# Paired weight products: two pieces split by one operation, a ring of eight half slots

## The reference

```
first block:   x += 0.5 * swiglu(rmsnorm(x))       w_gu 1024 x 5632, w_down 2816 x 1024
               x += hybrid_mixer(rmsnorm(x))       w_in; short convolution, gated linear attention,
                                                   sigmoid gates ga, gb, silu gate r, w_o
               x += 0.5 * swiglu(rmsnorm(x))
               x  = rmsnorm(x)
second block:  x += (neighbourhood attention | retention) @ w_out
               x += square(relu(rmsnorm(x) @ w_up)) @ w_down     4096 wide
               x  = rmsnorm(x)
```

## Time and profile before

| | before |
|---|---|
| median of three runs | 1752.6 us |
| profiled execution | 1752.49 us |
| its span | 1750.3 us |
| TensorE busy | 1743.7 us, 100% |
| VectorE busy | 1180.2 us, 67% |
| ScalarE busy | 847.5 us, 48% |
| GpSimd busy | 201.8 us, 12% |

### The profile page before, as it was taken

How to read it: one execution, slowest core, us unless ns; L and a number is a source line. 1 busy time by engine, 2 the same in 40 slices (tenths; PEclk the granted TensorE clock), 3 DMA queues, 4 the chain that set the end, 5 groups by cost and what they waited for, 6 DMA issues and landing times.

```text
span 1750.3 us, 26650 instructions
## 1 busy us (share of the span) xinstructions
PE 1743.7 (100%) x10407; PEld 1534.1 (88%) x10407; DVE 1180.2 (67%) x1843; ACT 847.5 (48%) x1442; POOL 201.8 (12%) x262
## 2 busy tenths in 40 slices
PE   9999999999999999999999999999999999999998
PEld 7889989878888899988888998988877888989897
DVE  7848748666776546865794784876688677747474
ACT  6425526454333335743553562654655543727274
POOL 1002201000001012200110220200232010202000
PEclk9999999999999999999999999999999999999999
DMA  7247736332125355733445573634522253637352
GB/s 224 79 139 173 195 97 157 110 108 86 51 85 155 97 145 154 175 107 98 136 121 152 147 193 111 167 100 133 139 62 61 85 144 97 161 109 185 100 133 72
DMA packets 85451, 220.66 MB, mean 126 GB/s; under 512 B 10800, under 2 KB 12080, under 8 KB 85328
## 3 DMA queue, kind: packets, MB, share of 16 engines
q1 hardware_dynamic: 58512, 156.92, 29.1%
q0 software_dynamic: 25536, 59.97, 16.0%
q10 hardware_dynamic: 1280, 2.08, 0.3%
HBM read 214.74 MB, written 2.10 MB: 124 GB/s over the span
## 4 chain that ended last, share of the span: by engine, by line
PE 97%; DVE 1%; ACT 0%; issue 0%; DMA 0%; DVEq 0%; ACTq 0%; POOLq 0%
PE ps L2101 19%; PE ps L2103 19%; PE ps L2102 19%; PE ps L2193 10%; PE ps L2195 10%; PE ps L2194 10%; PE ps L2123 2%; PE ps L2125 2%; PE ps L2124 2%; PE ps L2342 0%; PE ps L2472 0%; PE ps L2497 0%; PE ps L2483 0%; PE ps L2345 0%; PE ps L2330 0%
## 5 line engine op out<-in xcount | busy, mean ns | idle before, releaser
L2101 PE MATMUL ps<-Ahi,wh 128*128 128x512 f32 x913 | 357.1, 391 | 0.0
L2102 PE MATMUL ps<-Alo,wh 128*128 128x512 f32 x913 | 355.3, 389 | 0.0
L2103 PE MATMUL ps<-Ahi,wl 128*128 128x512 f32 x913 | 355.3, 389 | 0.0
L2193 PE MATMUL ps<-BThi,wh 128*128 128x256 f32 x1232 | 340.2, 276 | 0.0
L2194 PE MATMUL ps<-BTlo,wh 128*128 128x256 f32 x1232 | 340.1, 276 | 0.0
L2195 PE MATMUL ps<-BThi,wl 128*128 128x256 f32 x1232 | 340.1, 276 | 0.0
L585 ACT ACTIVATE wh<-raw 128x1024 fp32r<-128x1024 f32 (+1 forms) x206 | 213.2, 1036 | 221.1 <-PE ps L2103 187.1
L1203 DVE TENSOR_TENSOR wl<-raw,wh 128x1024 fp32r<-128x1024 f32 (+1 forms) x206 | 250.2, 1215 | 64.4 <-ACT wh L585 62.3
L2194 PEld LDWEIGHTS ps<-BTlo,wh 128*128 128x128 f32 x1232 | 231.3, 188 | 0.0
L2193 PEld LDWEIGHTS ps<-BThi,wh 128*128 128x128 f32 x1232 | 231.3, 188 | 0.0
L2195 PEld LDWEIGHTS ps<-BThi,wl 128*128 128x128 f32 x1232 | 231.2, 188 | 0.0
(11 more groups left out here) (398 smaller groups left out, 2802.9 us busy)
## 6 DMA issues: line engine op xcount, KB each, us to landing
raw<-in_w_gu SPq DMA_DIRECT2D x96, 256.0 KB, 3.1
raw<-in_w_d SPq DMA_DIRECT2D x32, 512.0 KB, 4.2
raw<-in_w_dn SPq DMA_DIRECT2D x32, 512.0 KB, 4.1
raw<-in_w_gu SPq DMA_DIRECT2D x22, 512.0 KB, 3.8
raw<-in_w_up SPq DMA_DIRECT2D x36, 256.0 KB, 2.9
SS<-in_w_gu POOLq DMA_DIRECT2D x32, 256.0 KB, 5.1
tm<-in_w_gu POOLq DMA_DIRECT2D x32, 256.0 KB, 4.0
S1B<-in_w_gu POOLq DMA_DIRECT2D x32, 256.0 KB, 5.1
```

Of the source, the lines that this page charges most:

```text
L2101: pe.matmul(ps, wh[:, c], hi[:, k, :], start=(k == 0), stop=False)
L2102: pe.matmul(ps, wh[:, c], lo[:, k, :], start=False, stop=False)
L2103: last = pe.matmul(ps, wl[:, c], hi[:, k, :], start=False, stop=(k == nb - 1))
L2193: pe.matmul(ps, whi[:, w], bhi, start=(new and kp == 0), stop=False, skip_group_check=not new)
```

## The change

The seven pieces of a pair become five splits: b11; s1 and s2 together; b12; s3 and s4 together; b22. `STEP` says which split a product belongs to. One ScalarE copy and one VectorE subtraction of 1024 columns serve two pieces. For that, s1 (two buffers, for even and odd pairs) and s2 lie in one tensor SUM1 of three rows, s3 and s4 in SUM3; an operation reads two of the three rows. The outputs lie in two neighbouring half slots, so a pair starts at an even slot from which neither double wraps round, and the slots before are skipped. The ring has eight half slots instead of six; one scratch row, S1B, S3B and SW3 fall away, and the descriptor scratch shrinks from 4096 to 2048 bytes. Because a double needs its second piece, the sums s2 and s4 stand ahead of the doubled high parts. TensorE's products and their order do not change, nor does SyncE's order.

Core of the diff:

```diff
-NW = 3
-NTMP = 9
+NW = 4
+NTMP = 8
+STEP = (0, 1, 1, 2, 3, 3, 4)
+NS = 5
...
-        i = ws % 6
+        i = ws % 8
...
+            while ws % 8 in (1, 3, 5, 6, 7):
+                slot(slot_free.get(ws % 8))
             got = [slot(p) for p in pens]
...
-            got = [raw(wns[c], 1) for c in (2, 4, 6)]
+            got = [raw(wns[k], 1) for k in (1, 3, 4)]
...
+    SUM1, _ = sb("SUM1", [P, 3, T])
+    SUM3, _ = sb("SUM3", [P, 3, T])
+    SS, SS2 = SUM1[:, 0, :], SUM1[:, 2, :]
...
+    def part(p, k):
+        if k in (1, 3):
+            return (SUM1, SUM3)[k // 2][:, PAIR[p] % 2:3:2 - PAIR[p] % 2, :]
+        return RAWP[RSL[p][k // 2]]
+    def split(t, p, k):
+        i = WS[p][STEP.index(k)]
+        if k in (1, 3):
+            return t[:, 512 * i:512 * i + 1024].rearrange("p (i n) -> p i n", i=2)
+        return t[:, 512 * i:512 * i + 512]
...
                 if TWOP[p] is not None:
                     pool.wait_ge(s["wl"], WN[TWOP[p]][1])
-                    pool.wait_ge(s["sd"], 2 * PAIR[TWOP[p]] + 1)
                 pool.dma_start(view(s1), block_of(p + 1, 0)).then_inc(s["sa"], 16)
                 if TWOP[p] is not None:
-                    pool.wait_ge(s["wl"], WN[TWOP[p]][4])
+                    pool.wait_ge(s["wl"], WN[TWOP[p]][3])
...
+            if k in (1, 3):
+                act.wait_ge(*added(p, k))
+                act.wait_ge(s["sd"], 2 * PAIR[p] + (k + 1) // 2)
             else:
-                act.wait_ge(s["sd"], 2 * PAIR[p] + {2: 1, 5: 2}[c])
-            act.wait_ge(s["pe"], WF[p][c])
-            act.activation(WHP[WS[p][c]], part(p, c), ACT.Copy).then_inc(s["wh"], 1)
+                act.wait_ge(s[f"raw{RSL[p][k // 2]}"], RN[p][k // 2])
+            if WF[p][k] > 0:
+                act.wait_ge(s["pe"], WF[p][k])
+            act.activation(split(WHF, p, k), part(p, k), ACT.Copy).then_inc(s["wh"], 1)
...
+                    if j == first:
+                        tap(p, 0)
+                        pair_hi(p, 3)
+                    else:
+                        pair_hi(p, 3)
+                        pair_a(j - 1, j - 1 - a)
+                        tap(p, 0)
                     pair_hi(p, 4)
-                    if j > first:
-                        pair_a(j - 1, j - 1 - a)
-                    tap(p, 0)
-                    pair_hi(p, 5)
-                    pair_hi(p, 6)
                     tap(p, 1)
...
+        def pair_lo(p, k):
+            dve.wait_ge(s["wh"], WN[p][k])
+            dve.tensor_tensor(split(WLF, p, k), part(p, k), f32(split(WHF, p, k)), ALU.subtract).then_inc(s["wl"], 1)
...
-                    pair_lo(p, 4)
+                    pair_lo(p, 3)
                     if j > first:
                         a_lo(38 * f + a, j - 1 - a, TA[4])
-                    pair_lo(p, 5)
-                    pair_lo(p, 6)
+                    pair_lo(p, 4)
                     if v in PAIR:
+                        total(v, 2)
                         pair_lo(v, 0)
-                        total(v, 2)
                     merge(p, 0, TA[2][:, LEFT])
-                    if v in PAIR:
-                        pair_lo(v, 1)
...
             for c, b in enumerate((0, 1, 0, 2, 0, 1, 0)):
-                pe.wait_ge(s["wl"], WN[p][c])
+                pe.wait_ge(s["wl"], WN[p][STEP[c]])
```

More of the change, by code:

```diff
@@ L217, in _counts @@
             pe += NP
-            wns = [w + c + 1 for c in range(NP)]
-            w += NP
+            wns = [w + k + 1 for k in range(NS)]
+            w += NS
+            while ws % 8 in (1, 3, 5, 6, 7):
+                slot(slot_free.get(ws % 8))
             got = [slot(p) for p in pens]
             WS.append([i for i, _ in got])
-            WF.append([f for _, f in got])
+            WF.append([max(f or 0 for (_, f), o in zip(got, STEP) if o == k) for k in range(NS)])
             WN.append(wns)
             PEN.append(pens)
-            got = [raw(wns[c], 1) for c in (2, 4, 6)]
+            got = [raw(wns[k], 1) for k in (1, 3, 4)]
             RSL.append([i for i, _, _ in got])
@@ L243, in _counts @@
         if ws % 2:
-            slot(slot_free.get(ws % 6))
+            slot(slot_free.get(ws % 8))
         i, free = slot(pe)
@@ L313, in build @@
     WLS, _ = sb("wl", [P, NW, 1024], F32R)
-    RAW, WH, WL = ([t[:, i // 2, :] for i in range(6)] for t in (RAWS, WHS, WLS))
-    RAWP, WHP, WLP = ([t[:, i // 2, 512 * (i % 2):512 * (i % 2) + 512] for i in range(6)] for t in (RAWS, WHS, WLS))
+    RAW, WH, WL = ([t[:, i // 2, :] for i in range(n)] for t, n in ((RAWS, 6), (WHS, 8), (WLS, 8)))
+    RAWP, WHP, WLP = ([t[:, i // 2, 512 * (i % 2):512 * (i % 2) + 512] for i in range(n)]
+                      for t, n in ((RAWS, 6), (WHS, 8), (WLS, 8)))
+    WHF, WLF = (t[:, :, :].rearrange("p i n -> p (i n)") for t in (WHS, WLS))
     R, _ = sb("R", [P, T])
[L317 to L320, removed]
+    SUM1, _ = sb("SUM1", [P, 3, T])
+    SUM3, _ = sb("SUM3", [P, 3, T])
+    SS, SS2 = SUM1[:, 0, :], SUM1[:, 2, :]
     TM = [sb(f"tm{i}", [P, T + 2])[0] for i in range(NTMP)]
+    at[0] += 56
     vec, _ = sb("vec", [P, NVEC])
@@ L384, in build @@
     BK = [PS[:, i, :] for i in range(8)]
-    TA = [t[:, 0:T] for t in TM]
-    RT = [SS[:, :], SS2[:, :], RS[:, :]]
+    TA = [t[:, 0:T] for t in TM] + [SUM3[:, 0, :]]
+    RT = [SS, SS2, RS[:, :]]
     G = [RQ[:, 0, :], RQ[:, 1, :], RK[:, 0, :], RK[:, 1, :]]
-    RET_S = [SS2[:, :], SS[:, :], RS2[:, :], RS3[:, :]]
+    RET_S = [SS2, SS, RS2[:, :], RS3[:, :]]
     RT_Q = [2, 1, 2, 0]
@@ L436, in sums_of @@
         odd = PAIR[p] % 2
[L437 to L443, removed]
+        return SUM1[:, odd, :], SUM1[:, 2, :], SUM3[:, odd, :], SUM3[:, 2, :]
+    def part(p, k):
[7 more added lines that the diff above has]
+        return t[:, 512 * i:512 * i + 512]
     def added(p, i):
@@ L585, in hi, with pair_hi @@
             act.activation(WH[WS[u]][:, 0:n], RAW[RSL[u]][:, 0:n], ACT.Copy).then_inc(s["wh"], 1)
[L587 to L593, removed]
[L594 to L597 removed]
+        def pair_hi(p, k):
+            if k in (1, 3):
+                act.wait_ge(*added(p, k))
+                act.wait_ge(s["sd"], 2 * PAIR[p] + (k + 1) // 2)
+            else:
+                act.wait_ge(s[f"raw{RSL[p][k // 2]}"], RN[p][k // 2])
+            if WF[p][k] > 0:
+                act.wait_ge(s["pe"], WF[p][k])
+            act.activation(split(WHF, p, k), part(p, k), ACT.Copy).then_inc(s["wh"], 1)
         def feed(u):
@@ L1221, in total @@
             if PREVP[p] is not None:
-                dve.wait_ge(s["wl"], WN[PREVP[p]][2 if i == 2 else 5])
-            if i == 4 and layer(p) == 3:
-                dve.wait_ge(s["bl"], 16)
+                dve.wait_ge(s["wl"], WN[PREVP[p]][1 if i == 2 else 3])
             if i == 4:
@@ L1249, in normed @@
             elif i > 0:
-                dve.wait_ge(s["wl"], WN[max(p for p in PAIR if layer(p) < i)][5])
+                dve.wait_ge(s["wl"], WN[max(p for p in PAIR if layer(p) < i)][3])
             halves = R[:, :].rearrange("p (h t) -> p h t", h=2)
@@ L1770, in dve_program @@
                 dve.wait_ge(s["rrow2"], 1)
-                own.add(dve.tensor_copy(SS2[:, :], BK[2][:, :]))
+                own.add(dve.tensor_copy(SS2, BK[2][:, :]))
                 own.wait()
@@ L1800, in dve_program @@
             for n in (2 * i, 2 * i + 1):
-                own.add(dve.scalar_tensor_tensor(out=X[:, n, :], in0=X[:, n, :], scalar=vc("gf", n), in1=SS2[:, :],
+                own.add(dve.scalar_tensor_tensor(out=X[:, n, :], in0=X[:, n, :], scalar=vc("gf", n), in1=SS2,
                                                  op0=ALU.mult, op1=ALU.mult))
```

118 lines of the change are left out of this document (46 added, 72 removed).

## The result

The changed kernel takes 1756.9 us (median of 11, 1756.6 to 1757.5); the kernel before, on the same chip, 1753.4 (1752.6 to 1754.0). The ratio is 1.0022, 95% interval 1.0013 to 1.0031: 3.5 us slower, 4.2 above the forecast and 0.9 above the range. The profiled execution of after took 1757.46 us with a span of 1755.4. It is the slowest of its eleven, and that of before (1752.49) is faster than all of its eleven, so the two spans lie further apart than the medians.

What follows compares the result with a forecast made beforehand. TensorE was taken as the bound, busy 1743.7 of 1750.3 us. Span 1750.3, plus 0.2 for waits at the two feed-forward entries, plus 2.19 around it, gave 1752.7 us; the 8-in-10 range was 1750.5 to 1756.0.

Steps and rivals of the forecast that it cites:

- the part on what is later: Paired units: operands made later by the doubled splits still reach TensorE in time, except small waits at two feed-forward entries.
- the steady pairs of the feed-forward layers: Pairs within feed-forward runs: later splits keep margins of 2.1, 3.0 and 2.3 us, so nothing reaches TensorE.
- my 0 to 0.3: First pair of each feed-forward layer: predicted wait in us at product 4; 0 to 0.6 in all, 0.2 taken.
- the mechanism was the one I gave: Feed-forward entries: the doubled high part waits for s4's late sum, delaying product 4's low part; 0 to 0.3 us each.
- another pace as a rival: Paired matmuls: moved buffer addresses change their pace, 4.7 us per ns, 1748 or 1757; chance slower 0.04, faster 0.05.
- Late sums: Rival at VectorE's sum s2: later DMA loads stall it and TensorE, 0.3 us on some 33 pairs, 1763; chance 0.07.

Runs made afterwards that it cites:

- e1: Changed kernel with, in the last MLP, product 0's PSUM copy put ahead of the doubled high part on ScalarE; 1758.7 us, ratio 1.0035.
- h: Kernel before with only the DMA descriptor scratch halved, 2048 instead of 4096; 1752.9 us against 1752.7, ratio 0.9999.
- l: Changed kernel with PSUM copies and s4's entry sums moved earlier, plus idle ScalarE copies (0.80, 1.04, 1.32 us) in the MLP runs' second pairs; 1756.2 us, 1.0017.
- i: Kernel before, single splits, last MLP: s3's high part moved to its own pair's start, s1's low part behind VectorE's second addition; 1756.1 us, 1.0018.
- e2: Changed kernel with, in the gates, product 2's PSUM copy put ahead of the high part that waits for the late gated row; 1756.1 us, 1.0020.
- e3: Changed kernel with s4's sum in both feed-forward layers' entry pairs made right behind the low part of s1 and s2; 1756.6 us, 1.0020.

## Why the prediction was wrong

**The step that failed** is the last sentence of the part on what is later: "In the gates and the last MLP the same order holds, with copies of rows in between that stand there already." I had worked out the steady pairs of the feed-forward layers, where indeed no product is late in after, and carried the result over. In the gates and the MLP other instructions stand between, each waiting for another engine. There the splits that are made later push VectorE's additions and gated rows, these hold up ScalarE, and ScalarE's queue holds up a PSUM copy. Eight of the nine late products are there, 3.2 of the 4.7 us.

**Behind it lies a second omission:** I asked of each product when its low part is ready. TensorE waits for a PSUM copy too, at products 2 and 4, and all nine late starts ended with a copy. The entry of feed-forward 2 shows the difference. I expected the doubled low part at 907.5, 0.2 ahead of product 4, and it was ready at 909.18 (907.95 + 1.23); the pair itself came 1.57 later than before, so this is 907.6. That sum was right. But product 2's copy, four instructions behind the double on ScalarE, was ready 0.3 later still, and product 4 waited 0.37 us. That this is near my 0 to 0.3 is luck, for the cause is another. At the first layer's entry the mechanism was the one I gave, the doubled low part, and cost 0.06; the slow spacing added 0.15.

**A term that was missing:** the slow spacing. I had another pace as a rival, by addresses, and gave it 0.04. It came behind hold-ups instead: 0.89 us at the second layer's entry and 0.15 at the first's in the profiled execution. I also had no term for the second matmul of a late product, 0.05 to 0.08 us at each of the nine.

**What was right:** TensorE's order and count; 112 operations fewer on both engines, and worth nothing. The doubles' durations, after's line 607 on ScalarE and 1209 on VectorE:

```profile
L607 ACT ACTIVATE wh<-SUM x112: 1040/1060/1072, 79.3 to 1692.5; 128x1024 fp32r<-128x1024 f32 x112
```

```profile
L1209 DVE TENSOR_TENSOR wl<-SUM,wh x112: 1211/1217/1227, 81.2 to 1693.6; 128x1024 fp32r<-128x1024 f32 x112
```

1060 and 1217 ns, where I took 1053 and 1237. The busy times came to 1155 and 834, against 1165 and 826 expected. Late sums did not come: no paired product of a steady feed-forward pair is late.

## What to carry to other kernels

Where one operation takes the place of two on an engine that executes in order, follow every instruction that moved behind it to the next thing that the bounding engine waits for, in each loop separately; here these were short copies out of PSUM and, but for one place, not the split operands. Put such copies first, where their input is ready, ahead of work with time to spare, and look for the next copy that this makes late, as in e1: with all of them in place the same doubled operations cost nothing that the runs could tell (0.9998, 0.9989 to 1.0007). Check it on the starts of the bounding engine's instructions, because a drawn duration that is longer than the distance between two starts hides short waits.

## What the runs showed of the hardware

A paired matmul of 256 columns starts 113.3 ns after the one before or 118, at a granted clock of 1.00 in both cases, and the slow spacing lasts over whole pairs, to the next plain units or in some cases to the next late start. It set in behind hold-ups of a product's first two matmuls of 0.04 us (h) to 0.6 us (the longest dose of l), not behind all: of the six late starts of i, three were followed by it, and the waits of 0.22 to 0.23 us in the MLP were followed by it at the third pairs of e2 and e3, but nowhere in after, whose MLP is the same. What decides it is open.

The Trainium skill (TensorE: Matmul & The Clock Gate, Wait — 56ns, not 53.3ns?) gives the columns at 2.4 GHz plus about 2.5 ns between the starts of warm matmuls (those at the upper level), by which 256 columns would take an estimated 109 ns. No stretch here has that: 113.3 is the fast spacing, 118 the slow one. In both kernels the gate pairs' products 0, 3 and 5, whose activations are read from other tiles than those of the other four products, take 118 to 119 ns a matmul at a granted clock of 1.00; no run here asked why.
